# A further pass's gate and up matmuls joined to the main pass, scatter landings awaited later

## The reference, cut to what matters

```
pg = softmax(t @ w_rg);  best of 4 groups
pe = softmax(t @ w_re in that group);  best 2 of 8    # e_w = e_prob / sum * g_prob
a = t @ w_g[e];  u = t @ w_u[e]                       # 1024 -> 256, 32 experts
y = sum over the two experts of  e_w * ((silu(a) * u) @ w_d[e])    # 256 -> 1024
```

## Time and profile before

| | |
|---|---|
| median of three runs | 1069.69 us (1067.76 to 1073.68) |
| profiled execution: its own time | 1068.85 us |
| profiled execution: span of the trace | 1067.0 us |
| PE busy | 834.5 us (78%) |
| DVE, ACT, POOL busy | 329.9, 165.9, 157.6 us |
| DMA | 318.11 MB, mean 298 GB/s |
| chain that ended last | PE 47%, DMA 37%, DVE 6%, issue 4% |

### The profile page before, as it was taken

One profiled execution on the slowest core, in us unless ns is written; L12 is line 12 of the kernel. 1 busy time (PEld: TensorE's weight loads), 2 busy tenths in 40 slices (PEclk: granted clock), 3 DMA queues, 4 the chain that ended last, 5 costly groups with the idle time before them and its releaser, 6 DMA issues.

```text
span 1067.0 us, 13800 instructions
## 1 busy us (share of the span) xinstructions
PE 834.5 (78%) x4921; PEld 442.0 (41%) x4922; DVE 329.9 (31%) x803; ACT 165.9 (16%) x354; POOL 157.6 (15%) x243
## 2 busy tenths in 40 slices
PE   3999999968977878879778855998489787777740
PEld 2556566645555323323233334664443233332310
DVE  3014554544744111111011128256511110111117
ACT  1121222232000110111110112110111111101110
POOL 1032030211101120111111101100101111111110
PEclk9999999989977998999899986999589999998985
DMA  9993652283597494999999889464659999999831
GB/s 337 365 349 129 214 181 91 88 358 114 202 376 283 165 384 193 418 420 421 420 420 411 328 317 369 173 260 170 257 216 420 420 420 421 418 420 406 367 128 75
DMA packets 90179, 318.11 MB, mean 298 GB/s; under 512 B 13087, under 2 KB 26111, under 8 KB 65561
## 3 DMA queue, kind: packets, MB, share of 16 engines
q1 hardware_dynamic: 70016, 274.60, 65.1%
q0 software_dynamic: 13312, 22.16, 5.9%
q10 hardware_dynamic: 6808, 20.79, 5.1%
HBM read 315.81 MB, written 26.80 MB: 321 GB/s over the span
## 4 chain that ended last, share of the span: by engine, by line
PE 47%; DMA 37%; DVE 6%; issue 4%; ACT 2%; SPq 2%; POOL 1%; POOLq 0%; DVEq 0%; ACTq 0%
DMA ring<-in_w_expert_up 24%; PE psum L905 14%; PE psum L788 8%; PE psum L734 6%; DMA ring<-in_w_ada 6%; PE psum L683 4%; PE psum L927 3%; DMA y_scratch<-arena,sidx 3%; DMA arena<-h_scratch,gidx 2%; DMA arena<-y_scratch 1%; PE psum L760 1%; PE psum L892 1%; SPq L365 1%; PE psum L1080 1%; PE psum L839 1%
## 5 line engine op out<-in xcount | busy, mean ns | idle before, releaser
L905 PE MATMUL psum<-ring,arena 128*64 128x512 f32 x1088 | 261.9, 637 | 58.5 <-DMA ring<-in_w_expert_up 54.6
L905 PEld LDWEIGHTS psum<-ring,arena 128*64 128x64 f32 x1088 | 94.0, 146 | 222.6 <-issue 220.3
L927 PE MATMUL psum<-ring,arena 128*64 128x512 f32 x544 | 124.2, 597 | 31.1 <-DVE arena L1655 29.8
L1651 DVE TENSOR_TENSOR arena<-arena,psum 128x256 f32<-128x256 f32 x34 | 14.3, 421 | 309.4 <-ACT arena L1204 309.4
L788 PE MATMUL psum<-ring,hT 128*128 128x384 f32 x288 | 98.2, 495 | 0.0
L927 PEld LDWEIGHTS psum<-ring,arena 128*64 128x64 f32 x544 | 39.7, 136 | 92.2 <-issue 76.7
L683 PE MATMUL psum<-ring,silu 128*32 128x128 f32 x1536 | 54.7, 302 | 26.1 <-DMA ring<-in_w_ada 25.6
L734 PE MATMUL psum<-ring,hT 128*128 128x512 f32 x160 | 70.3, 595 | 1.1 <-ACT hT L1277 0.7
L788 PEld LDWEIGHTS psum<-ring,hT 128*128 128x128 f32 x288 | 54.4, 194 | 35.0 <-issue 1.7
L1661 DVE COPY arena<-psum 128x512 f32<-128x512 f32 x34 | 23.5, 692 | 132.6 <-PE psum L927 132.6
L683 PEld LDWEIGHTS psum<-ring,silu 128*32 128x32 f32 x1536 | 47.5, 122 | 36.1 <-DMA ring<-in_w_ada 18.5
(11 more groups left out here) (176 smaller groups left out, 804.7 us busy)
## 6 DMA issues: line engine op xcount, KB each, us to landing
ring<-in_w_expert_gate SPq DMA_DIRECT2D x64, 1024.0 KB
ring<-in_w_expert_up SPq DMA_DIRECT2D x64, 1024.0 KB
ring<-in_w_expert_down SPq DMA_DIRECT2D x64, 1024.0 KB, 19.9
ring<-in_w_ada SPq DMA_DIRECT2D x24, 2048.0 KB, 15.6
ring<-in_w_qkv SPq DMA_DIRECT2D x9, 1024.0 KB, 12.3
arena<-m_scratch POOLq DMA_DIRECT2D x12, 512.0 KB, 7.3
h_scratch<-h ACTq DMA_DIRECT2D x6, 1024.0 KB, 10.2
arena<-y_scratch ACTq DMA_DIRECT2D x6, 1024.0 KB, 7.9
```

The lines of the kernel that those rows point to most:

```text
L905: last = pe.matmul(bank[b][64 * e:64 * e + 64, :].rearrange("p (g n) -> p g n", g=2), mem.GT[b][:, c, 64 * e:64 * e + 64], w, start=(c == ...
L927: last = pe.matmul(bank[5 + half][64 * e:64 * e + 64, :], mem.actT[b][:, f, 64 * e:64 * e + 64], w[:, f, 512 * half:512 * half + 512], sta ...
```

## The change

- **PE.** `passes` now takes four bodies: `begin` (gate/up of the main pass), and then either `alone` (no further pass; the order of before) or `joined` and `more`. `joined` does the transposes of the further rows, the main product's transposes, the further pass's gate/up, the main pass's down, and only then the transposes of the next pair's rows. `more` then does the further pass's product transposes and down (and whole passes from the second further one on). ScalarE and VectorE follow the same order; VectorE counts `gate_up_through` right behind the further up-multiply.
- **GpSimd.** `scatter` no longer waits for its landing. In each pair GpSimd gathers the further pass's rows first, then pair n+2's; then it waits for the landing of the scatter of pair n-1, counts O as free, and scatters pair n. With further passes it waits for this scatter's landing before it counts O free for the further one, and for the further scatter's landing behind it. The last landing is awaited behind the loop, and so is, in the first stage, that of `store_m`. A load of 512 bytes into a new tensor `landing` adds 16 to the scatters' semaphore ahead of the loop, in place of a landing before pair 0's.

The diff, without ScalarE's part, which splits its `first` and `body` in the same way as VectorE's:

```diff
@@ -158,6 +158,7 @@
         self.table = sb("table", [P, 8 * PAIRS], I32)
         self.sidx = sb("sidx", [P, 2], I32)
         self.gidx = sb("gidx", [P, 3], I32)
+        self.landing = sb("landing", [2, P])
         K = 256
         self.arena = a = sb("arena", [P, 50 * K])
 
@@ -304,7 +305,7 @@
         main = [moe_sems(f"main{l}") for l in range(2)]
         extra = moe_sems("extra")
 
-        def passes(eng, l, S, first, body):
+        def passes(eng, l, S, begin, alone, joined, more):
 
 
             eng.wait_ge(words_done, l + 1)
@@ -313,12 +314,15 @@
                 with eng.Fori(0, PAIRS // 4) as it:
                     for b in range(2):
                         n = half * (PAIRS // 2) + it * 2 + b
-                        first(n, b, half * (PAIRS // 4) + it)
                         times = eng.snap((word >> (it * 6 + 3 * b)) & 7, min_val=0, max_val=PASSES - 1)
+                        begin(n, b, half * (PAIRS // 4) + it)
                         with eng.If(times > 0):
+                            joined(n, b, half * (PAIRS // 4) + it, eng.snap(further[eng]))
                             with eng.Fori(0, times) as r:
-                                body(n, b, r + 1, eng.snap(further[eng]))
+                                more(n, b, r, eng.snap(further[eng]))
                                 eng.reg_add(further[eng], further[eng], 1)
+                        with eng.Else():
+                            alone(n, b, half * (PAIRS // 4) + it)
 
         further = {}
         block = ctx.enter_context(nc.Block())
@@ -567,7 +571,7 @@
             def scatter(S, l, col, n, b):
 
                 pool.tensor_copy(mem.sidx[:, b:b + 1], mem.table[:, bass.ds(col, 1)]).then_inc(S["sidx"], 1)
-                n1, n2, n16 = value(n + 1), value(n + 2), value(16 * n + 16)
+                n1, n2 = value(n + 1), value(n + 2)
                 pool.wait_ge(S["sidx"], n1)
                 pool.wait_ge(S["o_act"], n2)
                 pool.wait_ge(S["o_dve"], n2)
@@ -576,18 +580,18 @@
                                         bass.IndirectOffsetOnAxis(ap=mem.sidx[:, b:b + 1].bitcast(U32), axis=0),
                                         mem.O[b], None, bounds_check=out_bound, oob_is_err=False
                                         ).then_inc(S["scattered"], 16)
-                pool.wait_ge(S["scattered"], n16)
 
             stored = [0]
 
-            def store_m(l, first, last, ready):
+            def store_m(l, first, last, ready, landed=True):
 
                 pool.wait_ge(ada_done, ready)
                 for i in range(2):
                     pool.dma_start(m_dram[l, i].rearrange("(u j n) -> j u n", j=4, n=P)[:, first:last, :],
                                    mem.m[i:i + 97:32, l, first:last, :]).then_inc(m_out, 16)
                 stored[0] += 32
-                pool.wait_ge(m_out, stored[0])
+                if landed:
+                    pool.wait_ge(m_out, stored[0])
 
             def spread(dst, l, vec, i, done):
 
@@ -630,9 +634,10 @@
                 for m in range(2):
                     gather(S, l, m, m, m)
                 if l == 0:
-                    store_m(1, 4, 6, ADA_AT[1, 5])
+                    store_m(1, 4, 6, ADA_AT[1, 5], landed=False)
+                pool.dma_start(mem.landing[l:l + 1, :], A["k_rows"][0:1, 0:P]).then_inc(S["scattered"], 16)
                 pool.wait_ge(table_done, 2 * l + 2)
-                pool.sem_inc(S["o_free"], 2)
+                pool.sem_inc(S["o_free"], 1)
 
                 pool.wait_ge(words_done, l + 1)
                 with pool.Fori(0, 2) as half:
@@ -640,24 +645,33 @@
                     with pool.Fori(0, PAIRS // 4) as it:
                         for b in range(2):
                             n = half * (PAIRS // 2) + it * 2 + b
-                            n1 = value(n + 1)
+                            n1, n16, n32 = value(n + 1), value(16 * n + 16), value(16 * n + 32)
                             pool.wait_ge(S["gt_ps"], n1)
-                            gather(S, l, n + 2, n + 2, b)
+                            pool.sem_inc(turns, 1)
                             times = pool.snap((word >> (it * 6 + 3 * b)) & 7, min_val=0, max_val=PASSES - 1)
                             with pool.If(times > 0):
                                 gather(extra, l, PAIRS + n, pool.snap(further[pool]), 2)
+                            gather(S, l, n + 2, n + 2, b)
+                            pool.wait_ge(S["scattered"], n16)
+                            pool.sem_inc(S["o_free"], 1)
                             scatter(S, l, n, n, b)
-                            pool.sem_inc(turns, 1)
                             with pool.If(times > 0):
+                                pool.wait_ge(S["scattered"], n32)
+                                pool.sem_inc(turns, 1)
                                 with pool.Fori(0, times) as r:
                                     k = pool.snap(further[pool])
+                                    k16 = pool.snap(16 * k + 16)
                                     with pool.If(r > 0):
                                         gather(extra, l, (r + 1) * PAIRS + n, k, 2)
                                     pool.sem_inc(extra["o_free"], 1)
                                     scatter(extra, l, (r + 1) * PAIRS + n, k, b)
+                                    pool.wait_ge(extra["scattered"], k16)
                                     pool.sem_inc(turns, 1)
                                     pool.reg_add(further[pool], further[pool], 1)
-                            pool.sem_inc(S["o_free"], 1)
+                pool.wait_ge(S["scattered"], 16 * PAIRS + 16)
+                pool.sem_inc(S["o_free"], 1)
+                if l == 0:
+                    pool.wait_ge(m_out, stored[0])
                 for tiles in ([0], [1, 2]):
                     root(tiles)
                     if l == 0:
@@ -932,27 +946,42 @@
             def mlp(l):
                 S = main[l]
 
-                def first(n, b, it):
-
+                def begin(n, b, it):
                     slots = [2 * b + e for e in range(2)]
                     gate_up(S, n, b, slots, [(landed[i], 32 * (it + 1 + l * EXPERTS // SLOTS)) for i in slots])
+
+                def own_down(n, b, it):
+                    slots = [2 * b + e for e in range(2)]
+                    down(S, n, b, slots, [(down_landed[i], 16 * (it + 1 + l * EXPERTS // SLOTS)) for i in slots])
+
+                def alone(n, b, it):
                     gt(S, n + 1, 16 * it + (16, 32)[b], 1 - b)
                     act_transposes(S, n, b)
-                    down(S, n, b, slots, [(down_landed[i], 16 * (it + 1 + l * EXPERTS // SLOTS)) for i in slots])
-
-                def body(n, b, r, k):
+                    own_down(n, b, it)
+
+                def joined(n, b, it, k):
+                    gt(extra, k, 16 * k + 16, 2)
+                    act_transposes(S, n, b)
+                    gate_up(extra, k, b, [2 * b + e for e in range(2)], [])
+                    own_down(n, b, it)
+                    pe.wait_ge(extra["gt_act"], k + 1)
+                    pe.wait_ge(extra["gt_dve"], k + 1)
+                    gt(S, n + 1, 16 * it + (16, 32)[b], 1 - b)
+
+                def more(n, b, r, k):
                     slots = [2 * b + e for e in range(2)]
-                    pe.wait_ge(S["gt_act"], n + 2)
-                    pe.wait_ge(S["gt_dve"], n + 2)
-                    gt(extra, k, 16 * k + 16, 2)
-                    gate_up(extra, k, b, slots, [])
+                    with pe.If(r > 0):
+                        pe.wait_ge(S["gt_act"], n + 2)
+                        pe.wait_ge(S["gt_dve"], n + 2)
+                        gt(extra, k, 16 * k + 16, 2)
+                        gate_up(extra, k, b, slots, [])
                     act_transposes(extra, k, b)
                     pe.wait_ge(S["o_act"], n + 2)
                     pe.wait_ge(S["o_dve"], n + 2)
                     down(extra, k, b, slots, [])
 
                 gt(S, 0, 16, 0)
-                passes(pe, l, S, first, body)
+                passes(pe, l, S, begin, alone, joined, more)
                 pe.drain().then_inc(mlp_end, 1)
 
             def router(l, t):
...
@@ -1670,23 +1708,33 @@
                 S = main[l]
                 dve.sem_inc(S["o_dve"], 1)
 
-                def first(n, b, it):
-
+                def begin(n, b, it):
                     up_times(S, n, b)
+
+                def alone(n, b, it):
                     gt_evict(S, n + 1, 1 - b)
                     at_evict(S, n, b)
                     o_evict(S, n, b)
 
-                def body(n, b, r, k):
+                def joined(n, b, it, k):
                     gt_evict(extra, k, b)
+                    at_evict(S, n, b)
                     up_times(extra, k, b)
                     dve.sem_inc(gate_up_through, 1)
+                    o_evict(S, n, b)
+                    gt_evict(S, n + 1, 1 - b)
+
+                def more(n, b, r, k):
```

(6 more changed lines are left out.)

13 lines of the change are left out of this document (10 added, 3 removed).

## The result

The changed kernel takes 1075.22 us (median of 20 runs, 1071.83 to 1081.56), the kernel before 1071.04 us beside it (20 runs, 1067.76 to 1075.41). The ratio is 1.0037, with a 95% interval of 1.0024 to 1.0049: about 4 us slower. The forecast was 1062.5 us with 1055 to 1070 as its range, so the measured time lies outside the range, and the change made the kernel slower instead of faster.

The account below looks back on a forecast made before the run. The first expert stage was taken as bound by its weight stream: pair 4's reload 8.9 us earlier, less 1.7 idle DMA, gains 7.2. So 1068.85 - 7.2 = 1061.65, plus 0.84 for the median: 1062.5 us, range 1055 to 1070.

Parts of the forecast that it names:

- What bounds the stage, and pair 0 on PE: Expert stage lasts as long as its weight stream; pair 0's further rows usable at 348, reload 357.9, scatter 362.4.
- The queue of GpSimd, which sets pair 2: On GpSimd, scatter 0 lands at 369.5, further scatter 379.9; pair 2's further gather issued 385.0, landed 391.9.
- rival (a): Longer scatter and gather landings around pair 2 eat the gain, leaving 0.8 us, about 1069; chance 0.24 together with (d).
- PE then waits some 4.4 us: Ahead of pair 2's further pass PE idles 4.4 us, against 6.16 before; reload for pair 4 at 404.6.
- signs named for being wrong: Pair 4's reload past 410, plateaus over 16.2 us a pair, instruction packets inside a plateau, second-stage saving over 2 us.
- What is late next: Pair 4's down weights wait on scatter 2's landing until about 416.8; DMA idle 1.7 us, net gain 7.2 us.
- (d): Pair 2's rows stay late for another reason, reload near 413, time 1069 to 1070; chance 0.24 together with rival (a).
- Rival (c): PE's longer loop no longer stays on chip, costing fetches: 1077, or over 100 us slower; chance 0.10.
- next to nothing: Pair 0's regrouping on PE by itself hardly gains: pair 1's gate/up starts 0.45 us earlier.
- The rest: Pairs without a further pass: earlier gathers put at nothing, new branches cost nothing with 3.4 us to spare per pair.

Follow-up runs that it names:

- the first experiment: GpSimd's new order and late awaiting alone, with PE, ScalarE and VectorE as in the kernel before: 1063.3 us, ratio 0.9925.
- second experiment: The joined order on PE, ScalarE and VectorE alone, with GpSimd as in the kernel before: 1084.05 us, ratio 1.0126.
- rows ahead: Kernel after, with an own output buffer, dummy load at program start and further rows gathered one pair earlier: 1057.2 us, ratio 0.9867.
- third own-buffer kernel: Kernel after, with an own output buffer for further passes and the new dummy load at the program's start: 1065.3 us, ratio 0.9944.
- first own-buffer kernel: Kernel after, with an own output buffer for further passes and its dummy load just ahead of the expert stage: 1067.51 us, ratio 0.9967.

## Why the prediction was wrong

- **What bounds the stage, and pair 0 on PE: right.** Further rows usable at 348.76 (348 forecast), reload at 358.63 (357.9), scatter 0 at 362.99 (362.4).
- **"The queue of GpSimd, which sets pair 2": the step that failed.** The order of instructions was right, the landings in it were too small. Scatter 0 held the queue until 373.98 (369.5 forecast), the further scatter until 384.36 (379.9), and the gather went out at 389.76 instead of 385.0. It then took 10.85 us to usable rows, where I took 6.9 and allowed 8.5 as the most. Rows at 400.61 instead of 391.9: 8.7 us, all but 0.2 of what the forecast saved ahead of the reload, and it is in these three landings: 3.9, 0.3 and 3.9 us too short, with 0.6 from scatter 0's later start; the steps between them agree. I had put scatter 0's landing between an idle and a loaded one because its weights "end near 368", and rival (a) was marked down because "the pair 2 stream has a pause just there". The pause came, but later: full traffic ran until 371, and GpSimd was released at 373.98, at the pause's end. The further scatter and the gather then ran beside weights, which went on until about 398.
- **A gather asked beside weights takes longer than one asked at their end.** Asked at 389.76 it was usable at 400.61; asked at 395.98 before, at 400.79, because the traffic ebbs at about 398 and the landing took only 4.8 us. So the first microseconds of asking earlier bought nothing. Asking still earlier does pay: in the first experiment the gather went out at 384.33 and landed after 10.9 us, at 395.2, some 2 us before its stream ebbed. The kernel that asked at 372.18 had its rows after 10.3.
- **The down weights behind pair 0's reload: left out.** The forecast has the further eviction wait for scatter 0, and draws the price only at pair 4. But the same wait held the down weights until 373.99, 15.4 us behind the reload, and 3.7 us of traffic were lost. That is most of why the stream ended at about 398 as before, though it had begun 4.7 us earlier.
- **"PE then waits some 4.4 us": it waited 13.10.** The lower clock behind it was forecast rightly, though it held for all of the gate/up in two of three profiles (8.91 and 8.94 us) and only a small part in the first (7.37). With 7.37 the reload came at 78.1 from the first gather, with 8.9 at 79.9 and 80.1: no clear gain on the 79.8 to 81.2 of before. Two of the signs named for being wrong showed: a reload past 410 (411.57), and more than 16.2 us a pair (198.25 / 12 = 16.5), the latter from the late down weights at the plateau's start.
- **"What is late next": right in its mechanism, too small.** The down weights of pair 4 waited on scatter 2, as said; 8.86 us of blocked eviction, and 2.7 us of traffic lost instead of 1.7. What I left out: pair 5's gather stands behind the same landings, and costs PE 4.76 us and slow transposes, though under full traffic and so without loss for the stage.
- **Rival (a), the gain eaten by landings, was the right kind** and had 0.24 with (d). It stopped at 1069 because I bounded each landing by the longest of before, took nothing for pair 0's down weights, and made the hole ahead of pair 4's too small.
- **Rival (c), my slower case, was wrong.** The page has 29 instruction packets in q8 instead of 27, one more in each stage, and between 420 and 600 us the list of queues again has none. The kernel did get slower, which had a chance of 0.10, but by another mechanism, and one that I had as a detail: the joined order alone costs 13 us (second experiment). I had priced the order change at "next to nothing" because I set only PE's times side by side, and put the later scatter into a queue whose landings I took as short.
- **"The rest", in the pairs without a further pass: right** to within 0.5 us in the mean.

The Trainium skill ("DMA: Bandwidth & Descriptors", Anatomy of one DMA — SWDGE (gpsimd) path) gives a DMA issued by GpSimd about 2.0 us and its bytes at 436 GB/s. The 24 indirect transfers between 420 and 600 us of the kernel after moved 3.55 MB, 148 KB each, and for such a one the page's figures make an estimate of 2.3 us. The traces come near it only where the DMA is idle (3.24 us, 406.73 to 409.97, in the second experiment); beside weights they show 10.85.

The same page (Queues, rings and completion order) says that a completion's increment lands only after every earlier write of its DMA engine, in all its queues, and that an engine takes turns between its queues packet by packet. Either would hold a small transfer back behind weights; no run here tells the two apart.

**The stage behind the reload, over all fourteen profiles.** From the reload of pair 4 to the end of stage 1 the kernels take 208.3 to 208.7 us where its down weights follow 5.2 behind (210.1 in two), 211.4 to 211.7 where they follow 8.9 behind, and 213.1 to 215.1 where they follow 13.9 behind. Three parts make this up:

```
down weights behind the reload     5.2              8.9              13.9
last pair's gate/up starts at      193.7 to 194.1   194.8 to 195.1   198.2 to 198.5
  takes                            7.1, or 8.8      8.8              7.1, or 8.8
  and the last scatter follows in  7.5              7.8              7.8
```

So the order with its blocked eviction costs some 4.4 us of the stream, of which 1.0 is there without the block too. The 1.7 us of a slower last gate/up go with the granted clock of that stretch, and occur in every column, in the second one in all three profiles.

**What stays open.** Of the step of 3.4 us between the second and third column, 2.7 are the lost traffic; the rest I can't assign. Why scatter 0 was released only at 373.98, when the traffic had fallen since 371, no run here shows.

## What to carry to other kernels

Moving a gate/up ahead of a down moves every output of that pass back, and with it whatever waits for its landing: follow the scatter, its landing, the buffer it frees and the weights behind that, before counting what the reload gains. A small transfer that is asked beside a saturated weight stream should be priced at the longest landing of the trace and more. Moved from the stream's end into the stream, it can lose in its landing what it gains in its start; ask it earlier by more than that, ahead of the landings that block its queue. Test the halves of a two-part change alone: here one took 8 us off and the other added 13.

## What the runs showed of the hardware

- The further gather of pair 2 took, from issue to landing, 10.85 us in the kernel after, 10.9 with GpSimd's part alone, 11.8 with late awaiting alone, 10.3 with rows ahead, 9.4 in the third own-buffer kernel (386.65 to 396.05), 4.8 before, and 3.24 with the DMA idle: more than a factor of three for the same rows. The page's maximum of 8.5 for this line was no bound.
- A late landing is paid twice, by the wait and by the clock. Behind waits of 4.08, 6.65 and 13.10 us PE ran its transposes in 1.97 us instead of 1.16, and the gate/up in 9.76, 8.95 and 7.37 (8.9 in the other profiles) instead of 7.09. The granted clock in the idle time was 0.50. A wait of 2.38 us in the first own-buffer kernel was enough for slow transposes (351.36).
- The same 32 matmuls differ between profiles of one kernel: pair 0's gate/up took 7.09, 7.09 and 8.78 us in the three of before, the last pair's 7.09, 8.78 and 8.78 in those of after. One profile alone can mislead by 1.7 us there, as in the 81.21 of the table above.
- A load of 512 bytes, with weights moving, held GpSimd's queue for 5.63 us.
